# Head 0 read back in the last projection slab, masks built in the first stage, and a routing chain one step shorter in a mixer and mixture-of-experts kernel

## What is computed

```
mod = silu(c) @ w_ada + b_ada                    # six vectors sh1 sc1 g1 sh2 sc2 g2
h = rms_norm(x, norm1_w) * (1 + sc1) + sh1
q, k, v, f_logit, gb, gc, u = split(h @ w_in)    # 8 heads of 64; gb, gc, u of 512
qh, kh = rms_norm(q), rms_norm(k)                # per head
attn = softmax(qh kh' / 8 + cum_i - cum_j, causal) @ v    # cum = cumsum(log_sigmoid(f))
conv = gb * causal_short_conv(gc * u, conv_w)    # 3 taps
mixed = concat(rms_norm(attn, wa), rms_norm(conv, wc))
x = x + g1 * (mixed @ w_out)
h2 = rms_norm(x, norm2_w) * (1 + sc2) + sh2
logits = h2 @ w_router + b_router                # 32 experts, the best 4 of each token
x = x + g2 * sum over its 4 experts of weight * expert(h2)
```

## Time and profile before

| | us |
|---|---|
| median of 3 runs | 2427.46 (2427.1 to 2430.07) |
| the profiled execution's own time | 2427.8 |
| its span, first to last instruction | 2426.2 |
| PE busy | 2246.3 |
| DVE busy | 1752.6 |
| ACT busy | 1284.3 |
| POOL busy | 794.6 |

### The profile page before, as it was taken

The page is one execution under the profiler, slowest core; times in us unless marked ns, Lnnn a source line. Parts: engine busy times, 40 slices in busy tenths (PEclk is TensorE's granted clock), DMA queues, the critical chain, the costliest instruction groups (busy, mean ns, idle before and its releaser), DMA issues.

```text
span 2426.2 us, 37494 instructions
## 1 busy us (share of the span) xinstructions
PE 2246.3 (93%) x10569; PEld 1817.2 (75%) x10570; DVE 1752.6 (72%) x2230; ACT 1284.3 (53%) x1723; POOL 794.6 (33%) x780
## 2 busy tenths in 40 slices
PE   6899995886972999999999999999999999999997
PEld 2679883775861888888888888878888887878876
DVE  1684424664673699986679967687999768789697
ACT  2332211664322577765567755565777556567575
POOL 1253003893035143342223322231332422133142
PEclk9899997998985999999999999999999999999999
DMA  7134203982232799996669977696999977799695
GB/s 242 64 126 144 69 1 100 257 221 85 105 122 90 276 350 364 378 338 230 223 229 374 366 264 230 225 302 223 375 371 363 317 227 253 271 321 373 239 346 175
DMA packets 299173, 583.98 MB, mean 241 GB/s; under 512 B 23841, under 2 KB 53553, under 8 KB 297009
## 3 DMA queue, kind: packets, MB, share of 16 engines
q1 hardware_dynamic: 269200, 501.68, 59.3%
q0 software_dynamic: 26560, 69.06, 10.5%
q10 hardware_dynamic: 3362, 12.59, 1.4%
HBM read 544.79 MB, written 44.24 MB: 243 GB/s over the span
## 4 chain that ended last, share of the span: by engine, by line
PE 60%; DVE 4%; issue 2%; DVEq 1%; POOL 1%; ACT 0%; DMA 0%; POOLq 0%; ACTq 0%
PE psum L1925 54%; DVE d_wlo L1759 3%; PE psum L1907 3%; PE psum L1869 2%; PE psum L1877 2%; DVE d_up L1772 0%; DVE d_act L1778 0%; DMA d_xg<-xn_d,d_entry 0%; POOL d_colf L1581 0%; DVE d_y_two L1749 0%; ACT d_y_two L1661 0%; DVE d_atlo L1784 0%; DVEq L1445 0%; DVEq L1444 0%; DVEq L1443 0%
## 5 line engine op out<-in xcount | busy, mean ns | idle before, releaser
L1759 DVE TENSOR_TENSOR d_wlo<-d_raw,d_whi 128x1024 fp32r<-128x1024 f32 x578 | 673.7, 1218 | 77.1 <-ACT d_whi L1636 76.1
L1636 ACT ACTIVATE d_whi<-d_raw 128x1024 fp32r<-128x1024 f32 x578 | 574.6, 1053 | 113.1 <-PE psum L1925 88.9
L1925 PE MATMUL psum<-d_whi,d_xthi 128*128 128x512 f32 x1152 | 458.7, 398 | 0.1
L1925 PE MATMUL psum<-d_whi,d_xtlo 128*128 128x512 f32 x1152 | 454.6, 395 | 0.0
L1925 PE MATMUL psum<-d_wlo,d_xthi 128*128 128x512 f32 x1152 | 454.5, 394 | 0.0
L1550 POOL DMA_INDIRECT out_dram<-d_yst,d_dest x49 | 93.0, 1897 | 808.8 <-DVE d_yst L1806 752.1
L1759 DVE TENSOR_TENSOR d_wlo<-slab,d_whi 128x1024 fp32r<-128x1024 f32 x292 | 343.4, 1217 | 4.2 <-ACT d_whi L1636 2.4
L1636 ACT ACTIVATE d_whi<-slab 128x1024 fp32r<-128x1024 f32 x292 | 292.5, 1054 | 6.0 <-PE psum L1925 5.6
L1925 PEld LDWEIGHTS psum<-d_whi,d_xtlo 128*128 128x128 f32 x1152 | 216.9, 188 | 50.7
L1925 PEld LDWEIGHTS psum<-d_whi,d_xthi 128*128 128x128 f32 x1152 | 217.0, 188 | 49.9 <-issue 1.5
L1925 PEld LDWEIGHTS psum<-d_wlo,d_xthi 128*128 128x128 f32 x1152 | 217.3, 189 | 48.4
(11 more groups left out here) (304 smaller groups left out, 3964.4 us busy)
## 6 DMA issues: line engine op xcount, KB each, us to landing
slab<-in_w_gate_up_dram SPq DMA_DIRECT2D x144, 1024.0 KB, 7.6
d_raw<-in_w_gate_up_dram SPq DMA_DIRECT2D x144, 1024.0 KB, 9.0
d_raw<-in_w_down_dram SPq DMA_DIRECT2D x144, 1024.0 KB, 6.9
b_wp<-in_w_ada_dram POOLq DMA_DIRECT2D x16, 1024.0 KB, 8.6
slab<-in_w_in_dram SPq DMA_DIRECT2D x12, 1024.0 KB, 5.4
slab<-in_w_ada_dram SPq DMA_DIRECT2D x8, 1024.0 KB, 5.1
b_q<-q_d SPq DMA_DIRECT2D x24, 256.0 KB, 7.7
b_k<-k_d SPq DMA_DIRECT2D x24, 256.0 KB, 8.6
```

The costliest lines, as they stand in the source:

```text
L1636: nc.scalar.activation(whi[n % NW][:, part, :], raw[n % NRAW][:, part, :], ACT.Copy).then_inc(whi_ok, 1)
L1759: nc.vector.tensor_tensor(wlo[n % NW][:, part, :], raw[n % NRAW][:, part, :], whi[n % NW][:, part, :].bitcast(F32), ALU.subtract).then_inc ...
L1925: mm = nc.tensor.matmul(to, m_[:, KH * h + k, :], w_[n % NW][:, k, :], start=(h == 0 and k == 0 and q == 0), stop=(h == 1 and k == KH - 1 ...
```

## The change

- The buffers `whi[1]`, `wlo[1]` of the projection are now the shared tile pair `s.early`, which is also buffer 0 of `q1`, `k1`, `q2`, `k2`. When PE is done with slab 11, SP loads head 0's q and k into it and POOL writes the zeros, while slab 12 is multiplied. The attention block starts with the v of head 0 and the loads of head 1; DVE writes only buffer 1's zeros, after its second row minimum.
- `mask`, `ident_r` and `fold` are made by POOL at the start of the projection.
- The roots of the convolution's norm stay in `s.crs`. Their reciprocals are made in 8 pieces of 128x128 by DVE in the attention, one a head (`conv_rstd`), and the scaling in the mixer, 4 instructions of 128x128 a block, at the head of `attention_norm`. ACT's `cthi` waits for it (`cn_ok`).
- The mixer's order changes. PE: `project(t)` piece 0 (36 matmuls), `turn_norm(t-1)`, `turn_attention(t+1)`, `project(t)` piece 1 (12 matmuls), `logits(t-1)`, `positions(t-2)`. DVE: `attention_norm(t+1)`, `attention_lo(t+1)`, `residual(t)`, `place(t-2)`, `norm2(t)`, `choose(t-1)`. ACT: `h2(t-1)` before `attention_hi(t+1)`. The steps end at t = 9 and not 10.
- `entry` is filled once by POOL for all blocks, and `place` writes its 4 slots with one instruction where 17 stood.
- The count is made from `sel_before` and the last `sel` in two matmuls right after the last positions.

```diff
-        whi = [sb(f"a_whi{i}", [P, KT, SW], F32R) for i in range(2)]
-        wlo = [sb(f"a_wlo{i}", [P, KT, SW], F32R) for i in range(2)]
+        whi, wlo = ([sb("a_" + n, [P, KT, SW], F32R), held.rearrange("p a (k n) -> p (a k) n", n=SW)]
+                    for n, held in (("whi", s.early[0]), ("wlo", s.early[1])))
...
+                sp.wait_ge(unit_mm, last_unit[len(slabs) - 2] + 1)
+                for i in range(2):
+                    sp.wait_ge(q_st[i], 16 * NQK)
+                q1, k1, q2, k2 = (s.early[n // 2][:, n % 2, :].bitcast(F32) for n in range(4))
+                for dst, src in ((q1[0:HD, :], s.q_d[0, 0:HD, :]), (q1[HD:P, :], s.q_d[1, 0:HD, :]),
+                                 (k1[0:HD, :], s.k_d[0, 0:HD, :]), (k1[HD:P, :], s.k_d[0, 0:HD, :]),
+                                 (q2[0:HD, :], s.q_d[0, 0:HD, :]), (k2[0:HD, :], s.k_d[1, 0:HD, :])):
+                    sp.dma_start(dst, src).then_inc(early_in, 16)
+                sp.wait_ge(pad_ok, 1)
+                sp.wait_ge(ext_st, 16 * 8)
+                for dst, src in ((q2, s.extq_d), (k2, s.extk_d)):
+                    sp.dma_start(dst[HD:HD + 4, :], src[0, :, :]).then_inc(early_in, 16)
+                sp.wait_ge(early_in, 16 * 8)
...
+                    if k == 2 * CT - 4:
+                        pool.wait_ge(unit_mm, last_unit[len(slabs) - 2] + 1)
+                        pool.wait_ge(csq_ok, k)
+                        nc.gpsimd.memset(s.early[1][HD:P, :, :].bitcast(F32), 0.0).then_inc(pad_ok, 1)
+                        pool.wait_ge(pad_ok, 1)
...
-                dve.wait_ge(csq_ok, 2 * CT)
-                for h in range(2):
-                    dve.wait_ge(rstd_ok, NQK + 1 + h)
-                    own.link(nc.vector.reciprocal(rstd[h][:, :], rstd[h][:, :]))
-                    for ct in range(CT):
-                        part = slice(h * HALF, (h + 1) * HALF)
-                        own.link(nc.vector.scalar_tensor_tensor(s.convn[:, ct, part], s.convn[:, ct, part],
-                                                                cnw[:, ct:ct + 1], rstd[h][:, :], ALU.mult, ALU.mult))
...
+                def conv_rstd(n):
+                    part = s.crs[:, n // 4, n % 4 * P:(n % 4 + 1) * P]
+                    nc.vector.reciprocal(part, part)
...
+                    if n == 1:
+                        for x in (q2, k2):
+                            nc.vector.memset(x[1][HD:P, :].bitcast(F32), 0.0).then_inc(pad_ok, 1)
...
+                    if c % 12 == 3:
+                        conv_rstd(c // 12)
...
-                pe.wait_ge(const_ok, 4)
...
+                    act.wait_ge(cn_ok, i + 1)
                     nc.scalar.activation(cthi[b][:, :, :], s.convn[:, :, bass.ds(i * P, P)], ACT.Copy).then_inc(athi_ok, 1)
...
+                    tokens = bass.ds(i * P, P)
+                    for ct in range(CT):
+                        part = s.convn[:, ct, tokens]
+                        ins = nc.vector.scalar_tensor_tensor(part, part, s.cnw[:, ct:ct + 1], crs[:, tokens],
+                                                             ALU.mult, ALU.mult)
+                    ins.then_inc(cn_ok, 1)
                     dve.wait_ge(ars_ok, i + 1)
...
-                    for r in range(K4):
-                        nc.vector.tensor_copy(slot[b][r][:, :], slotf[:, K4 + r:K4 + r + 1])
-                        nc.vector.tensor_copy(entry[b][r][:, 0:1], tokf[:, bass.ds(i, 1)])
-                        nc.vector.tensor_copy(entry[b][r][:, 1:2], tokf[:, bass.ds(i, 1)])
-                        ins = nc.vector.tensor_scalar(entry[b][r][:, 2:3], tokf[:, bass.ds(i, 1)], float(K4), float(r),
-                                                      ALU.mult, ALU.add)
-                    own.link(ins)
+                    own.link(nc.vector.scalar_tensor_tensor(slot[b][:, :], topf[:, :], float(T), slotf[:, 0:K4],
+                                                            ALU.mult, ALU.add))
...
-                    if there(t - 3):
-                        place(t - 3, 1 - b)
                     if there(t - 2):
-                        choose(t - 2, b)
+                        place(t - 2, b)
                     if there(t):
                         norm2(t, b)
+                    if there(t - 1):
+                        choose(t - 1, 1 - b)
...
-                        project(t, b)
+                        project(t, b, 0)
+                    if there(t - 1):
+                        turn_norm(t - 1, 1 - b)
                     if there(t + 1):
                         turn_attention(t + 1, 1 - b)
+                    if there(t):
+                        project(t, b, 1)
                     if there(t - 1):
-                        turn_norm(t - 1, 1 - b)
+                        logits(t - 1, 1 - b)
                     if there(t - 2):
-                        logits(t - 2, b)
-                    if there(t - 3):
-                        positions(t - 3, 1 - b)
```

131 lines of the change are left out of this document (67 added, 64 removed).

## The result

The changed kernel took 2412.82 us (median of five runs, 2409.95 to 2417.4), the kernel before in the same sitting 2427.46 (five runs, 2426.48 to 2431.77): a ratio of 0.9935, 95% interval 0.9923 to 0.9948. It is 14.6 faster where 20.6 was forecast, and inside the forecast's range (2397 to 2416). The profiled execution took 2412.82, with a span of 2411.2.

The account below looks back on a forecast made before the run. Each block before the experts was bound differently: the projection's end by DVE's tail, the attention by DVE's last write, the mixer by PE. -19.2 + 9.8 - 11.2 = -20.6 gave 2406.9 us for the median, range 2397 to 2416.

Parts of the forecast that it names:

- Projection's end: End of the projection: without the DVE tail ACT's root is last, and the next block starts at 388.6, 11.2 earlier.
- Attention: Attention block: POOL ends it at 550.6 and the mixer starts at 551.5, 19.2 earlier including the projection's 11.2.
- a third by the forecast: Attention: share taken of the uncovered DVE reciprocals and zeros, between nothing and 7.6 + 2, giving an end at 548.
- Mixer's loop: Mixer's steps: two projections 15.8 apart against 14.35 before; first to eighth 106.1 against 98.0; together +9.8 with added terms.
- The wait of 1.45: Mixer's loop: PE stands 1.45 in each step (0.85 to 3.1) because `an` comes at 12.75 and PE arrives at 11.3.
- Tail: From the last projection's last matmul to the experts: 33.5 in place of 44.7, so -11.2.
- No stall: Rival, mixer: norm and choice come 1.45 sooner and PE never stands; 2399.0, chance 0.12.
- The attention ends last, not POOL: Rival, attention's end: uncovered reciprocals and late head 1 loads end it 4 to 6 later than POOL; about 2411.5, chance 0.13.
- POOL and DVE block each other: Rival, attention: the wider reciprocals wait out half of a POOL piece each, 18 in all; about 2428, chance 0.02.
- The clock falls in the stalls: Rival, mixer: PE goes on at the lower clock after each stall, 7.0 a step, 42 in all; 2449, chance 0.03.
- The early loads hold the projection open: Rival, projection's end: the moved loads last until DVE's old end, 8 earlier in place of 19.2; about 2418, chance 0.01.
- Experts: Experts' stretch: forecast unchanged, 0, since nothing in it is touched.

Follow-up runs that it names:

- the loads on SyncE: The changed kernel with eight gate-sum stores in the projection and the loads of pieces 2 to 15 in the attention issued by SyncE, not GpSimd: 2404.34 us.
- the same work one instruction further on: The changed kernel with the 32 scalings of 128x128 moved from the mixer to the attention, four behind each reciprocal: 2457.86 us, 1.0116 of before.
- VectorE's ballast: The changed kernel with two unused reciprocals of 128x512 added on VectorE behind its last multiplication in the projection: 2409.89 us.

## Why the prediction was right, and where it was not

**Projection's end: -11.2 forecast, -7.0.** The step that failed is "the last thing in the projection is ACT's root, and with the same 1.26 the next block starts at 388.6". The 1.26 were read as the barrier's fixed price. They were the price when VectorE is last; GpSimd's drain, 384.8 to 391.0, stood in the trace of before and was not asked for. With it the sum would have been 391.0 + 1.0 = 392.0. This is 3.4. The other 0.7 is the projection itself, whose last root starts at 387.38 and not 386.66; that lies inside the scatter by the clock (below). No trace shows that anything waited for the early loads, the new waits or the masks, as forecast; the 0.79 of one tensor_scalar cost nothing that shows either. What they might cost below that scatter, 3.8, these runs cannot tell.

**Attention: -8.0 forecast, -3.3.** The mechanism was right: GpSimd is late next. The reciprocals took 0.94 each where a line gave 0.95. TensorE's and VectorE's side was 157.3 long against 156.1 before, but over eight executions with the same attention it was 155.8 to 163.9, so what of the reciprocals and the zeros lay uncovered, a third by the forecast, cannot be read from it. Three terms were mis-sized. The first piece came 14.7 behind the start, not 12.8: 1.9, which the text allowed with "a microsecond or two" for v, head 1 and half of `w_out`, which are now loaded against it. That these loads are the reason was not tried; it was 14.4 to 16.2 in all eight executions. From the first piece's start to the last one's end 150.5, not 149.2: 1.3. And behind its last piece GpSimd drains for 1.44, so the block's end took 2.44 and not 0.88: 1.5.

**Mixer's loop: right.** Five steps of 15.8 forecast, 15.07, 15.82, 15.84, 16.41 and 15.84 measured; from the first to the eighth projection 105.5 against 106.1. The wait of 1.45 was 0.57 to 1.85, the four scalings 1.13 for 1.3. Taking 2.6 off VectorE's chain removed the wait (14.3 to 14.5), taking 1.1 off it left up to 0.76 (14.3 to 15.3), so it is shown to be a wait for that chain. Until the first projection's last matmul it took 0.3 more than before, not 1.7. This is luck: the first turn of `an` came 0.8 later and one more turn (0.44) stands ahead, but the first projection's matmuls took 1.0 less, with a granted clock of 0.82 from that first turn on against 0.76. In the second execution of the changed kernel it was 0.77, and the stretch took 1.25 more than before.

**Tail: -11.2 forecast, -13.5.** 31.2 from the last projection to the experts, not 33.5. GpSimd's last but one group of four came at 16.0 for 17.0, the last DMA at 25.2 for 26.2, and from there it took 6.01 for 7.29: its queue reached the block's end 1.2 behind the last DMA's end, 2.5 before, and its drain of 2.67 is the same in both. In the other executions with the new `place` it reached it 1.2 to 2.4 behind, so this too may be scatter.

**The rivals.** *No stall*: false, TensorE stood in five turns. *The attention ends last, not POOL*: false, but true with the loads on SyncE. *POOL and DVE block each other*: false for this change, since its reciprocals took 941 to 943 ns all eight times, and true for the same work one instruction further on, where it costs 56. *The clock falls in the stalls*: false; around the wait of 1.29 the granted clock is 1.00, and the matmuls behind it come each 0.23:

```profile
653.00:654.50 1.50, 0.59 (x5) 0.59 (x6) 1.35 (x2) 1.48 (x2) 0.00 (x0) 1.00 0.43 177
```

*The early loads hold the projection open*: false, they were issued by 364.4, SyncE, which waits for all eight, was at the block's end at 369.8, and GpSimd's drain ended it.

**Experts: 0 forecast, +1.1.** Twelve executions of the changed kernel and its edits with the same experts' work took 1676.0 to 1677.9 here, the one of before 1675.8. Whether that is more than chance stays open.

## What to carry to other kernels

When a tail is cut off a block, list for each engine when it would be ready, with the drain that its queue does at the block's end, and not only its last instruction; what a barrier costs depends on who is last. If an engine ends a block with work of its own, look for what is not work in it: here the issue of each load cost it 0.88. A reorder that shortens a chain at the end by a step can put that step into every pass of the loop, as the choice did here (8.8 off the tail, 8.8 on the loop); price the two ends apart, and move whatever nobody waits for behind the instruction that somebody does. And before a gain of a microsecond or two is put down to an edit, look how far the same stretch scatters where nothing was edited.

## What the runs showed of the hardware

**GpSimd's drain** at a block's end took 0.082 for each DMA it issued in the block: 0.30 for 3, 1.44 for 17, 2.67 for 32, 5.53 for 67, on top of what was still running. After 293 it took 4.88, so the line is not to be carried on.

**VectorE beside GpSimd.** The 128x128 scalings, 0.30 to 0.35 in the mixer, took up to 4.65, those of tensor_scalar (0.28) up to 4.53; the reciprocals from SBUF (0.94), and VectorE's instructions of the attention that read PSUM, kept their time.

**The projection scatters by the clock.** In 60 to 110 us the granted clock differs between executions in which nothing of that stretch was changed, and the block's last root starts between 384.5 and 388.3. Over all 14 executions the two go together: 0.90 (three) with a root at 384.5 to 384.9, 0.83 (eight) with 386.1 to 387.4, 0.80 (three) with 386.7 to 388.3. Before, after, and with VectorE's ballast:

```profile
60.00:110.00 50.00, 39.87 (x158) 29.98 (x159) 33.05 (x42) 17.56 (x30) 5.04 (x5) 0.80 0.19 61
```
```profile
60.00:110.00 50.00, 38.99 (x156) 29.43 (x157) 32.89 (x41) 16.98 (x29) 5.25 (x5) 0.83 0.18 57
```
```profile
60.00:110.00 50.00, 39.00 (x169) 29.66 (x170) 34.48 (x43) 18.61 (x33) 6.67 (x7) 0.90 0.19 62
```

These 3.8 are a part of the 3 to 10 between the slowest and the fastest run of one kernel, and the reason why the stages were compared from their own starts.
